# Spreading the top-value rounds of a hybrid decoder layer: one beside each recurrent group and three beside each attention head, in place of two and two

## The reference

```
proj = einsum('bsd,de->bse', rmsnorm(x), w_in)
xa, ga, q, ckv, gb, qi, ki, wi = split(proj)
# recurrence: conv of width 4, two gates, scan
ya = lru(conv(xa)) * silu(ga)
# indexer: score[q, s] = sum over 16 heads of wi * relu(qi . ki)
_, sel = top_k(where(causal, score, neg), 256)
logits = q_abs . c[sel] * HEAD_DIM ** -0.5 + rel_bias
yb = softmax(logits) . c[sel] . w_uv * silu(gb)
out = rmsnorm(x + concat(ya, yb) . w_out)
```

## Time and profile before

| what | value |
|---|---|
| median of 3 runs | 1465.3 us (1463.8 to 1465.96) |
| the profiled execution | 1463.75 us |
| its span, first to last instruction | 1461.9 us |
| granted TensorE clock, mean | 0.997 |
| PE busy | 1437.4 us (98%) |
| DVE busy | 1067.0 us (73%) |
| ACT / POOL busy | 634.5 us / 752.0 us |

### The profile page before, as it was taken

The page is one execution under the profiler, slowest core; times in us unless marked ns, Lnnn a source line. Parts: engine busy times, 40 slices in busy tenths (PEclk is TensorE's granted clock), DMA queues, the critical chain, the costliest instruction groups (busy, mean ns, idle before and its releaser), DMA issues.

```text
span 1461.9 us, 21789 instructions
## 1 busy us (share of the span) xinstructions
PE 1437.4 (98%) x7320; PEld 1278.4 (87%) x7320; DVE 1067.0 (73%) x1704; ACT 634.5 (43%) x917; POOL 752.0 (51%) x637
## 2 busy tenths in 40 slices
PE   8999999999999999999999999999999999999996
PEld 7899999988888888888888888888888888888885
DVE  6478666588789888878754566647878791899947
ACT  7345555543544534542211111145656443453563
POOL 5364454458788898885444444310000354556580
PEclk9999999999999999999999999999999999999998
DMA  8212111145545555546632222253443553354376
GB/s 287 87 51 79 44 50 43 29 137 156 165 141 175 183 182 160 176 138 206 202 122 57 87 93 93 83 174 125 149 154 94 176 165 102 101 170 148 100 248 263
DMA packets 181446, 197.15 MB, mean 135 GB/s; under 512 B 14614, under 2 KB 144776, under 8 KB 180360
## 3 DMA queue, kind: packets, MB, share of 16 engines
q1 hardware_dynamic: 179848, 192.16, 41.6%
q0 software_dynamic: 1536, 4.20, 0.9%
HBM read 141.26 MB, written 55.05 MB: 134 GB/s over the span
## 4 chain that ended last, share of the span: by engine, by line
PE 88%; DVE 6%; issue 2%; DMA 2%; ACT 2%; POOL 1%; SPq 0%; DVEq 0%; ACTq 0%
PE ps L1375 18%; PE ps L1376 18%; PE ps L1377 18%; PE ps L1624 5%; PE ps L1626 5%; PE ps L1625 5%; PE ps L1614 4%; PE ps L1495 2%; PE ps L1497 2%; PE ps L1595 2%; DMA wo_raw<-in_w_out 1%; PE ps L1387 1%; DVE rt L2149 1%; PE ps L1589 1%; PE ps L1588 1%
## 5 line engine op out<-in xcount | busy, mean ns | idle before, releaser
L1375 PE MATMUL ps<-hT_hi,w_lo 128*128 128x512 f32 (+1 forms) x1344 | 496.4, 369 | 0.0
L1377 PE MATMUL ps<-hT_hi,w_hi 128*128 128x512 f32 (+1 forms) x1344 | 495.8, 369 | 0.0
L1376 PE MATMUL ps<-hT_lo,w_hi 128*128 128x512 f32 (+1 forms) x1344 | 495.8, 369 | 0.0
L966 POOL TENSOR_TENSOR w_lo<-w_raw,w_hi 128x512 fp32r<-128x512 f32 x168 | 225.1, 1340 | 344.5 <-ACT w_hi L1051 344.4
L1375 PEld LDWEIGHTS ps<-hT_hi,w_lo 128*128 128x128 f32 x1344 | 254.1, 189 | 29.8
L1376 PEld LDWEIGHTS ps<-hT_lo,w_hi 128*128 128x128 f32 x1344 | 254.1, 189 | 29.7
L1377 PEld LDWEIGHTS ps<-hT_hi,w_hi 128*128 128x128 f32 x1344 | 254.0, 189 | 29.2
L1051 ACT ACTIVATE w_hi<-w_raw 128x512 fp32r<-128x512 f32 x168 | 104.6, 627 | 372.2 <-PE ps L1377 305.2
L995 POOL TENSOR_TENSOR wo_lo<-wo_raw,wo_hi 128x512 fp32r<-128x512 f32 x104 | 152.4, 1469 | 111.1 <-ACT wo_hi L1255 111.0
L955 POOL TENSOR_TENSOR w_raw<-w_raw,g_col 128x512 f32<-128x512 f32 x168 | 204.1, 1226 | 6.2 <-DMA w_raw<-in_w_in 6.2
L1891 DVE MATCH_REPLACE8 scores<-top,scores 128x384 f32<-128x384 f32 (+2 forms) x192 | 165.6, 873 | 0.0
(11 more groups left out here) (241 smaller groups left out, 2189.9 us busy)
## 6 DMA issues: line engine op xcount, KB each, us to landing
w_raw<-in_w_in SPq DMA_DIRECT2D x168, 256.0 KB, 2.8
tw<-in_w_out SPq DMA_DIRECT2D x128, 128.0 KB, 2.5
t_dram<-tw SPq DMA_DIRECT2D x128, 128.0 KB, 2.7
wo_raw<-t_dram SPq DMA_DIRECT2D x64, 256.0 KB, 2.6
wo_raw<-in_w_out SPq DMA_DIRECT2D x48, 256.0 KB, 3.2
xin<-in_x SPq DMA_DIRECT2D x8, 1024.0 KB, 6.9
out<-rt SPq DMA_DIRECT2D x12, 512.0 KB, 3.9
rt<-in_x SPq DMA_DIRECT2D x10, 512.0 KB, 5.0
```

The source lines that it names most:

```text
L966: nc.gpsimd.tensor_tensor(w_lo[:, j, :, :], w_raw[:, j, :, :], w_hi[:, j, :, :].bitcast(F32), ALU.subtract).then_inc(w_lo_s, 1)
L1375: nc.tensor.matmul(o, wlo, hi, start=(kt == 0), stop=False)
L1376: nc.tensor.matmul(o, whi, lo, start=False, stop=False)
L1377: return nc.tensor.matmul(o, whi, hi, start=False, stop=(kt == KT - 1))
```

## The change

The number of rounds is no longer the same for groups and heads. The total stays 32: 8 times 1 and 8 times 3. Nothing else is edited, and the instructions of TensorE, ScalarE, GpSimd and SyncE and their order stay the same.

```
-            per = ROUNDS // (G + NH)
+            per, per_head = 1, 3
+            assert per * G + per_head * NH == ROUNDS
             with dve.Fori(0, G) as g:
                 step.enter(g, 2 + 12 * per + 4)
...
             for h in range(2):
                 if h == 0:
                     low_q(h)
-                top_rounds(per)
+                top_rounds(per_head)
                 if h == 1:
                     low_q(h)
                 finish_gate(h)
...
             with dve.Fori(2, NH - 1) as h:
-                step.enter(h - 2, 12 * per)
-                top_rounds(per)
+                step.enter(h - 2, 12 * per_head)
+                top_rounds(per_head)
                 low_q(h)
                 finish_gate(h)
                 step.leave(NH - 3)
-            top_rounds(per)
+            top_rounds(per_head)
             low_q(NH - 1)
             dve.wait_ge(wuv_st, 32)
```

## The result

The changed kernel takes 1493.35 us, median of 4 runs (1490.94 to 1494.62), beside 1465.3 us before; the ratio is 1.0191, with a 95% interval of 1.0179 to 1.0203. It is slower by 28 us; the forecast was 1491.8. The profiled execution took 1490.94 us with a span of 1489.1 us, 27.2 us above the profiled one of before in either number.

A forecast was written before the change was run, and what follows sets the result against it. PE was taken as the bound, busy 1437.4 of 1461.9 us. Tile 31's 15.7, the keys' 7.4 and the clock's 4.6 sum to 27.7 us, giving 1491.5, taken as 1491.8 us for the median; range 1486 to 1497.

The forecast's parts named there:

- What bounds the kernel: Whole kernel: PE is busy 1437.4 of 1461.9 us, so time rises by whatever makes PE wait.
- The removed rounds give 0: Groups: `th` is set by ACT, so the removed round only leaves 10.7 us idle ahead of it; gain 0.
- 15.7 us at tile 31: Heads 0 and 1: late `low_q(1)` delays tile 31 by 15.7 us, including about 2.4 us waited at tile 30.
- Heads 2 to 6 cost 0: Heads 2 to 6: margins of 5.7 us, then 6.7 us per head, so PE waits for nothing.
- 7.4 us at the keys: End of heads: `c_t` load queues behind `q_stores(7)`, so POOL ends late and PE begins the keys 7.4 us late.
- The clock, 4.6 us: Behind the long waits at tile 31 and the keys: the clock falls, costing 2.3 us each, 4.6 together.
- Rival 1: Behind the two long waits: the clock costs nothing, 1486.9 us, or is paid once, 1489.2; chance 0.17.
- Rivals 2 to 5: Keys' wait hidden (0.04); last group's stores earlier (0.03); rounds only fill idle time (0.02); further wait in heads (0.10).

The follow-up runs named there:

- e4_drop: Against the kernel before: one round per group, heads kept at two, so 24 rounds in all and 192 keys per query; 1464.25 us, ratio 0.9994.
- e5_after_again: The changed kernel itself, run again for comparison on the same chip as later variants; 1494.49 us, ratio 1.0200 to the kernel before.
- e1_order: Changed kernel with rounds of heads 0, 1 and 7 reordered, so the third no longer precedes a due hand-over; 1477.99 us, ratio 1.0083 to before.
- e7_latent_first: Changed kernel with the load of `c_t` issued ahead of `q_stores(7)`, not behind it; 1484.71 us, ratio 1.0134 to the kernel before.
- e9_order_all: e1_order with, in heads 2 to 6, `low_q(h)` moved behind one round and ahead of the other two; 1464.64 us, ratio 1.0001 to before.
- e3_front: Against the changed kernel: head 7 back to two rounds, group 0 two, heads 0 to 6 still three; 1483.74 us, ratio 1.0124 to before.
- e6_filled: Changed kernel with PE's two long waits filled with transposes, 100 ahead of tile 31 and 60 ahead of the keys; 1489.08 us, ratio 1.0165 to before.
- e8_four_rounds: Against the changed kernel: no rounds in the groups and four in each head; 1533.06 us, ratio 1.0459 to the kernel before.

## Why the prediction was right

**What bounds the kernel.** Right: but for 0.4 us, all of the loss in the trace is PE idle or at the low clock.

**The removed rounds give 0.** Right, shown by e4_drop; `th` waits for ACT for 10.7 us, the number given.

**15.7 us at tile 31.** Right: 15.9 us in the trace. The split was off: 11.5 us of idle time and not 13.3 ahead of the tile, because tile 30 itself ran its first 3 us at the low clock. I had counted only the two long waits as long enough for the clock to fall. In the second trace, e5_after_again, the clock did not fall there, and the idle time is 13.1 us. The late weights stayed covered: PE waits for no weights in the heads in any of these kernels.

**Heads 2 to 6 cost 0.** Right in this kernel. The reason given, a margin of 5.7 us for `low_q(2)`, held only because tile 33 was late by then; e1_order showed that without that lateness the same hand-over is 10.3 us late.

**7.4 us at the keys.** Right: 7.8 and 7.2 us in two traces of the changed kernel, in which the load of `c_t` took 7.1 and 6.5 us to ACT's start and not 6.6; e7_latent_first shows that the way was the one described, `q_stores(7)` ahead of the load.

**The clock, 4.6 us.** The size was an estimate from the start of the span. There the clock is recorded as full, so that no row shows the 2.3 us to be the clock's. Behind the two waits the loss is 3.7 us in the first trace and 5.6 in the second, and filling the waits gave back 5.4 us. That 4.6 lies between them is in part luck. The rule of the Trainium skill, page "TensorE: Matmul & The Clock Gate", section "Part 1: The HAM clock gate (the "warmup" mystery)", names two states and a return only after sustained work; the traces agree, with a granted clock of 0.50 until 3 to 6 us of matmuls had run. Rival 1, that it costs nothing or is paid once, is out.

**Rivals 2 to 5** did not occur: the keys did wait, the last group's stores did not come earlier, the rounds were not hidden, and no further wait stood in the trace. The sum was 27.7 us; the profiled executions differ by 27.2 and the medians by 28. Its terms were nearly as good as the sum: tile 31 and the keys cost 0.2 and 0.4 us more in the first trace, the clock 0.9 less, and the trace began 0.6 us ahead.

## What to carry to other kernels

Spreading background work by idle time per stage is not enough: ask for each hand-over how much work stands ahead of it since the last one that was met, and when its reader comes; e9_order_all has the distribution of the changed kernel and loses nothing, since no `low_q` there has more than four rounds between itself and the one before, as in the kernel before. Where six stood between `low_q(0)` and `low_q(1)` (the changed kernel), or nine between `low_q(0)` and `low_q(2)` with tile 31 in time (e1_order), PE waited. A lateness can hide another one behind it, so mending one hand-over may show the next (e1_order). In this kernel, which TensorE bounds, a wait cost its length and 1.5 to 3 us more where the clock fell in it.

## What the runs showed that I had not expected

A wait of 2.4 us can be enough for the clock to fall: ahead of tile 30 the first trace has PE idle from 694.88 and a clock of 0.53 in the microsecond from 697.00, some 2.2 us later, and so has the trace of e7_latent_first. In the second trace of the changed kernel, with an equal wait, tile 30's first matmul took 0.48 us and the clock did not fall, nor did it in e3_front and e6_filled. In e8_four_rounds it fell behind a wait of 1.9 us and not behind those of 1.5 and 2.2 us. In the long waits of the two traces of the changed kernel it fell 4.5 and 5.4, and 4.7 and 2.9 us after the end of the last matmul. So the length of a wait alone does not say whether, or when, the clock falls. The length of the slow stretch behind a wait differed as well, from 2.9 to 6.0 us over the kept traces.

The two traces of the changed kernel differ by 3.6 us. Of these, 2.4 lie ahead of `th`, where the rounds cost nothing; the slow clock adds about 1.8, and the shorter wait for the keys takes 0.6 away. What makes the stretch ahead of `th` vary, no run here asks.

In e1_order the masks stand beside POOL's `c_lo`. The first mask, 128x384, took 4.37 us, where all six together took 2.69 us in the kernel before. VectorE's and POOL's timelines of e1_order:

```profile
972.19 4.37 DVE L1970 TENSOR_SCALAR mask<-scores 128x384 bf16<-128x384 f32 x1
976.48 2.42 DVE L1970 TENSOR_SCALAR mask<-scores 128x512 bf16<-128x512 f32 x5
```

```profile
971.80 4.54 POOL L987 TENSOR_TENSOR hT_lo<-c_t,hT_hi 128x2048 fp32r<-128x2048 f32 x1 [11.34 <-ACT hT_hi L1201]
```

The mask ends when POOL's instruction ends, at about 976.6 and 976.3. The Trainium skill, page "SBUF — State Buffer", section "Who interferes with whom", says that VectorE and GpSimd share a pair of ports by an exclusive lock, which a VectorE instruction needs in its two-port modes or with two inputs in SBUF, and that whoever issues first holds it for the whole instruction. These rows agree. So do two other traces in which POOL's `c_lo` overlaps the masks: in e9_order_all the first mask takes 4.25 us and ends 0.2 us behind `c_lo`, and in e7_latent_first the six take 5.75 us. In the kernel before and in the changed one they do not overlap, and the six take 2.69 us. The delay comes with the overlap in all of these traces; that a port is the reason is the page's account, and no run here tests it. It cost PE nothing.
